# Odd layer: one store for several column blocks, a shorter boundary to the value projection, and an output projection that begins with the attention's half

## The chip, the cores and the metric

One core of one Trainium2 chip runs the whole program once per call. The metric is the device time in microseconds, from the first to the last instruction with what lies around them. Three runs of the kernel before gave a median of 3164.81 us, from 3162.14 to 3166.29.

## The reference, cut to what matters

Two layers of a decoder, for 2048 prompt positions and 8 sample tokens (2056 columns). The change lies in the second, the odd layer:

```python
proj = x @ w_in                      # 21 groups of 128 channels here, and a value projection of 1024
o_c  = stick_breaking(q_c, k_c, v_c) # attention, 512 channels; for the 8 samples over a paged cache
o_d  = gla_chunked(q_d, k_d, v_d, log_a)                      # gated recurrence, 512 channels
o_d  = o_d * rsqrt(mean(o_d * o_d) + eps) * gn_g              # per head of 128
out  = concat([o_c * silu(g_c), o_d * silu(g_d)]) @ w_out     # 1024 x 1024
x    = layer_norm(alpha * x + out)
```

The output projection sums over 1024 channels. The first 512 are the attention's and need nothing more when they are loaded; the last 512 need the norm of the recurrence and the gate.

## The kernel before, in words

The program is a chain of stages. Between two stages all engines meet: a stage ends when each engine has run its list of instructions, and then semaphores are cleared and the next stage begins. Buffers placed at fixed addresses, and some semaphores, outlive a stage, so that one stage can load or compute ahead for the next. Each engine's order is written out by hand.

A product in 32 bit is made of three TensorE passes over operands split into a high and a low part (`product`, lines 120 to 122: high by low, low by high, high by high). `high_part` is a copy (line 108), `low_part` a subtraction (line 113).

**Odd projection** (`project_odd`, tiles named po_). The weights of a group of 128 channels are multiplied with five blocks of columns (four of 412 and one of 408). There are 105 such slots, each of 24 matmuls, in the order of `ODD_GROUPS`; the first five share the loop over the contraction (`first`), and slots 5, 6 and 7 are all the last block, of three different groups. ScalarE evicts each slot's bank into one of four pieces of `po_o` (`evict`, line 1371) and issues its store (`store`, line 1310, 206 KB). Before it writes a piece it waits until the store of four slots ago has landed. Beside this runs the samples' attention. SP loads cache pages of keys for VectorE, and ScalarE loads pages of values for TensorE (line 2497, four pages of 256 KB, after the store of the same slot). For each sample the step goes: ScalarE's exponential at slot t, VectorE's clamp, ScalarE's logarithm at t+1 (line 2620), VectorE's maximum (line 2673), TensorE's triangle sum at t+2 (line 2559), VectorE's argument, ScalarE's exponential at t+3 (line 2625), TensorE's value sums from t+4 (line 2552). Here t is 22, 32, ... 92. The transposes that make the query rows (line 2577) come after slot 9 and need slot 7 evicted and VectorE's four memsets, which follow its split of weight group 4.

**Boundary to the value projection** (`project_values`, tiles pv_). When the last slot is done, SP issues `ValuesAhead.load`: tile 0 of x, four of eight slices of weights (`FRONT = 4`), tile 1 of x. Then it stores the samples' attention output into scratch `cat` (line 2534) and waits for it. The next stage begins with SP's other four weight slices, VectorE's split of tile 0 of x (`split_x`), then ScalarE's high parts and VectorE's low parts of the weights. TensorE starts when slice 0 is split. Tile 1 is split by VectorE after the last weight slice, and its low part is GpSimd's (line 113).

**Odd output projection** (`Tail`, tiles oo_). Block b of 256 columns holds `cat` with 8 slices: 0 to 3 the attention's, 4 to 7 the recurrence's. Weights are loaded and split, and block 0 is loaded, during the stage before (`gla_chunks`). In the stage itself TensorE first sums squares of the recurrence (`back(0)`, line 812), ScalarE makes the reciprocal root, VectorE scales (line 1120) and gates (line 1131) slices 4 to 7, and then `high(0)` and the low part split all 8 slices of tile 0. Only then `tile(0)` multiplies: 48 matmuls into two banks. `back(1)` and `tile(1)` follow. VectorE's order after that is: evict half of tile 0, scale block 1, evict the other half, split tile 2, normalise tile 0, evict tile 1, and so on.

Of the kernel before, what the change touches and what calls it, by code (L numbers as in the profile page):

```python
# [22 lines left out]
P = 128  # L23
D = 1024
KT = D // P
# [522 lines left out]
class Tail:  # L548
# [48 lines left out]
    def run(self):  # L597
        even = self.even
        with self.s as s:
# [19 lines left out]
            self.w_low = [s.sem("w_low_even"), s.sem("w_low_odd")]  # L619
            self.CST_B = 48 if even else 16  # L620
# [180 lines left out]
    def tensor(self, pe):  # L801
# [73 lines left out]
        def turned(t):  # L875
            if not self.even or t < 0:
                return
            h, n = t % 2, self.rows(t)
            pe.wait_ge(self.y_ok, t + 1)
            if t:  # L880
                pe.wait_ge(self.yT_ok, t)
            else:
                pe.wait_ge(self.lnc, 48)
            for k in range(KT):
                mm = pe.transpose(self.tr[:, k // 4, (k % 4) * P:(k % 4) * P + n], self.y[h][0:n, k * P:(k + 1) * P],
                                  self.idt[0:n, 0:n])
            mm.then_inc(self.tr_pe, 1)
        centre(0)
# [3 lines left out]
        if self.even:  # L892
            centre(1)
            glu(1, (0,))
        tile(0)
# [30 lines left out]

    def gpsimd(self, pool):
        def low(t):
            h, n = t % 2, self.rows(t)
            c = slice(h * P, h * P + n) if t < TT else slice(0, n)  # L930
            pool.wait_ge(self.c_high, t + 1)
            low_part(pool, self.cl[h][:, :, 0:n], self.cb[t // 2 % 2][:, :, c], self.ch[h][:, :, 0:n]).then_inc(self.c_low, 1)
        for t in range(1, TT + 1):
            low(t)
# [126 lines left out]
    def vector(self, dve):  # L1061
# [71 lines left out]
        def high(t):  # L1133
# [5 lines left out]
            high_part(dve, self.ch[h][:, :, 0:n], self.cb[t // 2 % 2][:, :, c]).then_inc(self.c_high, 1)  # L1139
# [48 lines left out]
        low_part(dve, self.cl[0][:, :, :], self.cb[0][:, :, 0:P], self.ch[0][:, :, :]).then_inc(self.c_low, 1)  # L1188
# [54 lines left out]
class Channels:  # L1243
# [7 lines left out]
    def __init__(self, s, xT, w, out, groups, banks, pinned=False):  # L1251
# [14 lines left out]
        self.kept = [s.sem(f"kept{n}") for n in range(self.PIECES)]  # L1266
# [3 lines left out]
        for t, (i, n, b) in enumerate(self.slot):  # L1270
            self.begin.setdefault(i, t)
        self.opens = {t: i for i, t in self.begin.items()}
        self.at = {(n, b): t for t, (i, n, b) in enumerate(self.slot)}

    def place(self, stage=None):
# [8 lines left out]
        self.ot = s.sb("o", [P, self.PIECES, BLK])  # L1284
        self.acc = [s.ps(f"acc{n}", [P, 512]) for n in range(self.banks)]

# [1161 lines left out]
def project_odd(nc, xT, w, z, cache_k, cache_v, table, bias, const, q_rows, cat, values_ahead):  # L2448
# [7 lines left out]
    with Stage(nc, "po") as s:  # L2456
# [16 lines left out]
         o_ev, o_pe, gate, out, stored) = (s.sem(n) for n in (  # L2473
             "cst", "tab", "q_tr", "q_ev", "q_st", "set", "prod", "k_used", "v_used", "biased", "exp", "cl", "ln",
             "sp", "tri_pe", "own", "arg", "att", "o_ev", "o_pe", "gate", "out", "stored"))
# [24 lines left out]
        def _(sp):  # L2500
# [33 lines left out]
            sp.dma_start(cat[0:4, :, SEQ:COLS].rearrange("n p c -> p n c"), oc[:, :, :]).then_inc(stored, 16)  # L2534
            sp.wait_ge(stored, 16)
# [51 lines left out]
        def _(act):  # L2587
# [8 lines left out]
            for t in range(TAIL):  # L2596
                if t < pj.slots:
# [6 lines left out]
                    pj.evict(act.copy, act, t, more)  # L2604
                    pj.store(act, t)
# [21 lines left out]
            for t in range(pj.slots - pj.PIECES, pj.slots):  # L2627
                pj.stored(act, t)

        @block.vector  # L2630
        def _(dve):
# [62 lines left out]
            for t in range(START, TAIL):  # L2694
# [10 lines left out]
                if t - PER - 3 in chain:  # L2705
# [4 lines left out]
                              gc[:, :, :].rearrange("p n b -> p (n b)"), ALU.mult).then_inc(out, 1)  # L2710

# [6 lines left out]
class ValuesAhead:  # L2718

    FRONT = 4  # L2720

    def __init__(self, nc, x, w):
# [9 lines left out]
        self.x_high, self.x_low = s.sem("x_high"), s.sem("x_low")  # L2732
# [8 lines left out]
    def load(self, sp):  # L2741
# [3 lines left out]
        self.tile(sp, 1)  # L2745
# [303 lines left out]
def project_values(nc, ahead, out, z, alpha_w, alpha_b, const, ops, wc, sample_vecs, scores):  # L3049
# [6 lines left out]
    with ahead.s as s:  # L3056
# [29 lines left out]
        def _(sp):  # L3086
# [43 lines left out]
            sp.wait_ge(late, 48)  # L3130
            for q in (0, 1):
# [104 lines left out]
        def _(dve):  # L3236
# [53 lines left out]
            ahead.split_x(dve)  # L3290
# [451 lines left out]
```

## Time and profile before

| | us |
|---|---|
| median of 3 runs | 3164.81 |
| the profiled execution's own time | 3165.45 |
| its span, first to last instruction | 3163.7 |
| TensorE matmul busy | 2913.2 (92%) |
| VectorE busy | 2101.6 (66%) |
| ScalarE busy | 1291.1 (41%) |
| mean granted TensorE clock | 0.969 |

The stages of the change lie at 1501 to 2137 us (odd projection), 2137 to 2348 (value projection) and 2936 to 3163 (odd output projection). Busy time is the union of an engine's instructions; an idle time in brackets stands before the instruction that ended it, with what released it.

### The profile page before, as it was taken

What the parts mean: (1) busy time and instruction counts of PE and PEld (TensorE: products, weight loads), DVE (VectorE), ACT (ScalarE), POOL (GpSimd) and SP (SyncE); (2) the same over time, 40 slices, a digit from 0 to 9 for tenths busy, and PEclk for the clock granted to TensorE, in tenths of its full rate; (3) what the DMA queues carried; (4) which work ended last, traced back from release to release, by engine and by line L of the source; (5) the groups of instructions that cost most, each with busy time, mean ns of one, the idle gap of its engine ahead of it and who ended that gap; (6) DMA issues with size and microseconds to landing.
All of it is one profiled execution on the core that took longest, in us unless ns stands there. A gap on an engine that the chain in (4) does not pass through costs nothing. (4 is left out here: it accounts for less than half of the span.)

```text
span 3163.7 us, 70060 instructions
## 1 busy us (share of the span) xinstructions
PE 2913.2 (92%) x27683; PEld 2367.9 (75%) x27683; DVE 2101.6 (66%) x3283; ACT 1291.1 (41%) x2293; POOL 724.9 (23%) x697
## 2 busy tenths in 40 slices
PE   8999999978898988998899999989989999998898
PEld 7899999967776766776887777877756666667676
DVE  9526666647666647885487677604639888887576
ACT  2225555434444435342310100012228888875332
POOL 5000000012232211110011111101227666664111
PEclk9999999989999989999999999999989999999999
DMA  6624545454443556552789999865450101008342
GB/s 214 204 95 151 154 151 153 140 162 117 105 116 87 130 150 195 158 174 84 260 253 342 319 330 322 294 192 170 149 193 6 68 14 55 15 20 257 124 158 77
DMA packets 470335, 502.83 MB, mean 159 GB/s; under 512 B 200065, under 2 KB 362866, under 8 KB 464986
## 3 DMA queue, kind: packets, MB, share of 16 engines
q1 hardware_dynamic: 373466, 339.83, 35.8%
q10 hardware_dynamic: 88032, 142.51, 13.0%
q0 software_dynamic: 8512, 16.02, 1.7%
q8 instruction: 221, 3.62, 0.5%
q14 instruction: 104, 0.85, 0.1%
HBM read 357.13 MB, written 141.31 MB: 158 GB/s over the span
## 5 line engine op out<-in xcount | busy, mean ns | idle before, releaser
L3029 POOL TENSOR_TENSOR sp_att<-sp_beta,sp_left 128x512 f32<-128x512 f32 (+3 forms) x320 | 302.3, 955 | 187.0 <-DVE sp_left L2990 172.6
L120 PE MATMUL po_acc<-po_x_high,po_w_low 128*128 128x412 f32 (+1 forms) x840 | 306.6, 365 | 15.1 <-DVE po_x_low L113 13.7
L120 PE MATMUL pe_acc<-pe_x_high,pe_w_low 128*128 128x412 f32 (+1 forms) x840 | 302.6, 360 | 5.4 <-PEq L86 5.4
L121 PE MATMUL po_acc<-po_x_low,po_w_high 128*128 128x412 f32 (+1 forms) x840 | 299.5, 357 | 0.0
L122 PE MATMUL po_acc<-po_x_high,po_w_high 128*128 128x412 f32 (+1 forms) x840 | 298.7, 356 | 0.0
L121 PE MATMUL pe_acc<-pe_x_low,pe_w_high 128*128 128x412 f32 (+1 forms) x840 | 293.7, 350 | 0.0
L122 PE MATMUL pe_acc<-pe_x_high,pe_w_high 128*128 128x412 f32 (+1 forms) x840 | 293.3, 349 | 0.0
L2990 DVE TENSOR_TENSOR_SCAN sp_left<-sp_z,sp_left,sp_zero 128x512 f32<-128x512 f32 x192 | 235.7, 1269 | 18.3 <-ACT sp_z L2951 14.0
L2654 DVE TENSOR_TENSOR po_work<-po_work,po_q 128x1024 f32<-128x1024 f32 x128 | 177.6, 1388 | 83.3 <-DMA po_work<-in_cache_k 74.4
L2943 ACT ACTIVATE sp_beta<-sp_z,sp_bias 128x512 f32<-128x512 f32 (+3 forms) x320 | 183.1, 628 | 94.1 <-PE sp_z L2881 47.7
L1371 ACT COPY po_o<-po_acc 128x412 f32<-128x412 f32 (+1 forms) x105 | 52.5, 500 | 392.2 <-PE po_acc L122 337.2
L120 PEld LDWEIGHTS po_acc<-po_x_high,po_w_low 128*128 128x128 f32 x840 | 162.4, 193 | 65.2 <-issue 33.1
L2430 POOL TENSOR_TENSOR rc_kt<-rc_kt,rc_mask 128x512 f32<-128x512 f32 x32 | 41.4, 1294 | 716.5 <-ACT rc_kt L2320 716.4
L2316 ACT COPY rc_lv<-rc_bk 128x1024 f32<-128x1024 f32 (+1 forms) x192 | 129.9, 693 | 181.1 <-DVE rc_f L2406 54.6
L2892 PEld LDWEIGHTS sp_t<-sp_id,sp_att 128*128 128x128 f32 x1088 | 117.4, 141 | 96.8 <-issue 89.8
L2951 ACT ACTIVATE sp_z<-sp_z,sp_bias_neg 128x512 f32<-128x512 f32 (+3 forms) x320 | 179.2, 610 | 0.0
L120 PEld LDWEIGHTS pe_acc<-pe_x_high,pe_w_low 128*128 128x128 f32 x840 | 158.4, 189 | 17.7 <-issue 16.5
L2878 PE MATMUL sp_z<-sp_k,sp_q 64*128 64x512 f32 (+3 forms) x640 | 164.0, 589 | 6.5 <-PEq L86 3.3
L2892 PE MATMUL sp_t<-sp_id,sp_att 128*128 128x128 f32 x1088 | 152.2, 279 | 17.5 <-ACT sp_aT L2957 16.6
L121 PEld LDWEIGHTS po_acc<-po_x_low,po_w_high 128*128 128x128 f32 x840 | 162.6, 194 | 0.9
L122 PEld LDWEIGHTS po_acc<-po_x_high,po_w_high 128*128 128x128 f32 x840 | 162.4, 193 | 0.7
L2909 PE MATMUL sp_ob<-sp_aT,sp_v 128*64 128x128 f32 x2176 | 154.7, 281 | 5.4 <-DVE sp_g L3004 5.4
(492 smaller groups left out, 6979.8 us busy)
## 6 DMA issues: line engine op xcount, KB each, us to landing
po_work<-in_cache_k SPq DMA_DIRECT2D x256, 256.0 KB, 4.8
po_work<-in_cache_v ACTq DMA_DIRECT2D x256, 256.0 KB, 4.6
scratch_ops<-pe_work SPq DMA_DIRECT2D x160, 128.0 KB, 2.0
out_z<-pe_o SPq DMA_DIRECT2D x84, 206.0 KB, 2.8
out_z<-po_o ACTq DMA_DIRECT2D x84, 206.0 KB, 4.2
pe_w<-in_w_e SPq DMA_DIRECT2D x21, 512.0 KB, 6.0
rc_opx<-scratch_ops SPq DMA_DIRECT2D x64, 160.0 KB, 3.7
po_w<-in_w_o ACTq DMA_DIRECT2D x20, 512.0 KB
```

Of the source, the lines that this page charges most:

```text
L120: pe.matmul(out, ll, rh, start=start, stop=False)
L121: pe.matmul(out, lh, rl, start=False, stop=False)
L122: return pe.matmul(out, lh, rh, start=False, stop=stop)
L2316: evict = lambda to, k, n: act.copy(lv[q][:, to:to + n].rearrange("p k x y c -> p x k (y c)"), b[:, :, 2 * k * CH:2 * (k + n) * CH].rearra ...
L2654: dve.tensor_tensor(kp[:, p % KR], kp[:, p % KR], qb[:, b % 2:b % 2 + 1, :].broadcast_to([P, 2, CW]), ALU.mult).then_inc(prod, 1)
L2878: mm[h] = pe.matmul(zb[h][b][:, 0:w], qt[q][r, cq], kt[q][r, ck], start=True, stop=not diagonal(n))
L2892: mm = pe.transpose(tb[h][:, b * P:(b + 1) * P], att[h][:, n % 3, b * P:(b + 1) * P], idt[:, :])
L2909: mm = pe.matmul(ob[tile(n) % 2][c, 0:P], vt[m % 2][:, 4 * g + b, c], aT[h][:, n % 2, b * P:(b + 1) * P], start=(diagonal(n) and b == 0), ...
L2943: act.activation(be[h][:, n % 4, 0:w], zb[h][n % 2][:, 0:w], ACT.Sigmoid, scale=DC ** -0.5, bias=bt[:, head:head + 1]).then_inc(sig[h], 1)
L2951: act.activation(zb[h][n % 2][:, 0:w], zb[h][n % 2][:, 0:w], ACT.Sigmoid, scale=-DC ** -0.5, bias=nbt[:, head:head + 1]).then_inc(kept[h], 1)
L2990: dve.tensor_tensor_scan(row[:, at:at + w][:, ::-1], zb[h][n % 2][:, 0:w][:, ::-1], zero.broadcast_to([P, w]), start, ALU.mult, ALU.add).t ...
L3029: pool.tensor_tensor(att[h][:, n % 3, 0:w], be[h][:, n % 4, 0:w], left[h][tile(n) % 2][:, at + 1:at + 1 + w], ALU.mult).then_inc(at_ok[h], 1)
```

## The change

1. Odd projection: `po_o` becomes one buffer of 2056 columns, with each block at its own columns. `runs` groups slots that follow each other in one weight group: blocks 0 and 1 make one store (412 KB), blocks 2 to 4 another (616 KB); a last block that stands alone is stored alone. `evict_run` waits for the latest store that covered this block.
2. Boundary: `FRONT` is 2, tile 1 of x is loaded in the next stage after the weights, the store of `cat` is waited for at the end of the next stage, and `split_x` is VectorE's last work in the odd projection.
3. Odd output projection: the attention's half of tile 0 (both halves of the output) and of tile 1 (the first) is split by VectorE before the norm, and multiplied by TensorE between `back(0)` and `tile(0)`. The later steps of these tiles take slices 4 to 7 only.

```diff
@@ Tail.tensor, tile(t)
-                if not self.even:
-                    pe.wait_ge(self.w_split, 2 * KT)
-                for k in range(KT):
+                for k in range(0 if self.even else 4, KT):
...
-                for k in range(KT):
+                for k in range(0 if self.even or u != 2 else 4, KT):
...
+        def attended():
+            pe.wait_ge(self.w_split, 2 * KT)
+            for t, halves in ((0, (0, 1)), (1, (0,))):
+                pe.wait_ge(self.a_low, t + 1)
+                for k in range(4):
+                    for q in halves:
+                        c = slice(q * 512, q * 512 + 512)
+                        product(pe, self.acc[2 * t + q][:, :], (self.ch[t][:, k, :], self.cl[t][:, k, :]),
+                                (self.wh[:, k, c], self.wl[:, k, c]), k == 0, False)
         centre(0)
         glu(0, (0,))
         back(0)
@@
+        else:
+            attended()
         tile(0)
@@ Tail: high and low parts of tiles 0 and 1 take these slices
+    def slices(self, t):
+        return slice(0, KT) if self.even or t > 1 else slice(4, KT)
@@ Tail.vector
+        def attended(t):
+            c, ks = slice(t * P, t * P + P), slice(0, 4)
+            if t == 0:
+                dve.wait_ge(self.b_in[0], self.loaded(0))
+            high_part(dve, self.ch[t][:, ks, :], self.cb[0][:, ks, c]).then_inc(self.a_high, 1)
+            dve.wait_ge(self.a_high, t + 1)
+            low_part(dve, self.cl[t][:, ks, :], self.cb[0][:, ks, c], self.ch[t][:, ks, :]).then_inc(self.a_low, 1)
@@
+        else:
+            attended(0)
+            attended(1)
         normed(0)
@@ Channels
+    def runs(self):
+        row, latest = [], {}
+        for t, (i, n, b) in enumerate(self.slot):
+            self.run_past[t] = latest.get(b)
+            row.append(b)
+            after = self.slot[t + 1] if t + 1 < self.slots else None
+            if after == (i, n, b + 1) and row != [0, 1]:
+                continue
...
+    def store_run(self, eng, t):
+        if t in self.run_end:
+            first, last = self.run_end[t]
+            lo, hi = first * BLK, min(COLS, (last + 1) * BLK)
+            eng.wait_ge(self.evicted, t + 1)
+            eng.dma_start(self.out[self.slot[t][1], :, lo:hi], self.ot[:, lo:hi]).then_inc(self.kept[first], 16)
+
+    def evict_run(self, copy, eng, t, more=()):
...
+        if self.run_past[t]:
+            first, count = self.run_past[t]
+            eng.wait_ge(self.kept[first], 16 * count)
+        eng.wait_ge(self.done, t + 1)
...
+        copy(self.ot[:, lo:hi], bank[:, 0:hi - lo]).then_inc(self.evicted, 1)
@@ project_odd, SP
-            sp.dma_start(cat[0:4, :, SEQ:COLS].rearrange("n p c -> p n c"), oc[:, :, :]).then_inc(stored, 16)
-            sp.wait_ge(stored, 16)
+            sp.dma_start(cat[0:4, :, SEQ:COLS].rearrange("n p c -> p n c"), oc[:, :, :]).then_inc(values_ahead.cat_put, 16)
@@ project_odd, ScalarE
-                    pj.evict(act.copy, act, t, more)
-                    pj.store(act, t)
+                    pj.evict_run(act.copy, act, t, more)
+                    pj.store_run(act, t)
@@ project_odd, VectorE, its last line
+            values_ahead.split_x(dve)
@@ ValuesAhead
-    FRONT = 4
+    FRONT = 2
@@ ValuesAhead.load
-        self.tile(sp, 1)
@@ project_values, SP
             for k in range(ahead.FRONT, KT):
                 ahead.weights(sp, k)
+            ahead.tile(sp, 1)
@@ its end
+            sp.wait_ge(ahead.cat_put, 16)
@@ project_values, VectorE
-            ahead.split_x(dve)
```

## Rows read from the trace of the kernel before

**Rows 1.** Windows of two stages: us, busy us of each engine (instructions), clock, DMA, GB/s.

```profile
1535.00:2125.00 590.00, 556.47 (x3017) 477.71 (x3015) 368.50 (x323) 61.37 (x137) 70.53 (x36) 0.97 0.86 288
2980.00:3163.00 183.00, 174.33 (x724) 131.04 (x724) 133.93 (x155) 58.14 (x84) 29.07 (x13) 0.98 0.37 122
```

**Rows 2.** Waits of PE, 1535 to 2125: engine, line, tile <- releaser: us, times, longest.

```profile
PE po_stat L2559 <- DVE po_softplus L2673: 15.5, 8, 6.5
PE po_sums L2552 <- ACT po_att L2625: 14.7, 7, 2.9
PE po_sums L2552 <- DMA po_work<-in_cache_v: 1.9, 2, 1.1
```

**Rows 3.** Timeline of ACT, one step of the odd projection: start us, duration, what [idle before].

```profile
1811.23 0.50 ACT L1371 COPY po_o<-po_acc 128x412 f32<-128x412 f32 x1
1811.76 0.36 ACTq L1310 DMA_DIRECT2D out_z<-po_o  x1
1812.83 3.78 ACTq L2497 DMA_DIRECT2D po_work<-in_cache_v  x4
1816.71 0.42 ACT L2620 ACTIVATE po_softplus<-po_e 128x256 f32<-128x256 f32 x1 [4.99 <-issue]
```

**Rows 4.** Timeline of PE at the two waits of the same sample.

```profile
1818.30 0.70 PE L2559 MATMUL po_stat<-po_softplus,po_tri 128*128 128x256 f32 x2 [1.51 <-DVE po_softplus L2673]
...
1831.61 1.06 PE L2552 MATMUL po_sums<-po_work,po_att 128*8 128x512 f32 x8 [2.04 <-ACT po_att L2625]
```

**Rows 5.** Windows after these two waits.

```profile
1818.00:1821.00 3.00, 2.71 (x15) 1.47 (x16) 3.00 (x2) 0.00 (x0) 2.41 (x1) 1.00 1.05 394
1833.00:1836.00 3.00, 3.00 (x14) 2.92 (x15) 2.13 (x2) 0.00 (x0) 0.00 (x0) 0.62 1.00 354
```

**Rows 6.** Timeline of PE near the stage's begin.

```profile
1561.56 0.60 PE L2577 MATMUL po_stat<-po_id,po_qc 128*8 128x128 f32 x4
```

**Rows 7.** Timeline of SP's queue at the boundary to the value projection.

```profile
2124.65 0.55 SPq L2736 DMA_DIRECT2D pv_x<-scratch_x1T  x1
...
2128.35 2.85 SPq L2534 DMA_DIRECT2D scratch_cat<-po_oc  x1
2137.85 1.76 SPq L2739 DMA_DIRECT2D pv_w<-in_w_v  x4
```

**Rows 8.** Windows at the same boundary.

```profile
2128.00:2132.00 4.00, 0.00 (x0) 0.00 (x0) 0.00 (x0) 0.00 (x0) 0.00 (x0) 0.84 1.06 412
2136.00:2138.00 2.00, 0.00 (x0) 0.00 (x0) 0.11 (x1) 0.14 (x1) 0.00 (x0) 0.50 0.00 0
```

**Rows 9.** Landings of the value projection's tiles of x, min/median/max.

```profile
DMA to landing us min/median/max: 4.2/4.8/8.7
```

**Rows 10.** Timeline of DVE and PE at the begin of the value projection.

```profile
2139.76 9.17 DVE L113 TENSOR_TENSOR pv_w_low<-pv_w,pv_w_high 128x1024 fp32r<-128x1024 f32 x8
...
2141.12 0.77 PE L120 MATMUL pv_acc<-pv_w_high,pv_x_low 128*128 128x512 f32 x1 [13.72 <-DVE pv_w_low L113]
```

**Rows 11.** Timeline of PE in the last stage.

```profile
2936.79 3.38 PE L812 MATMUL oo_part<-oo_rstd,oo_ones 128*128 128x512 f32 x4 [4.88 <-PEq L86]
2946.99 0.80 PE L120 MATMUL oo_acc<-oo_w_high,oo_cat_low 128*128 128x512 f32 x1 [6.82 <-DVE oo_cat_low L113]
...
2949.72 0.48 PE L120 MATMUL oo_acc<-oo_w_high,oo_cat_low 128*128 128x512 f32 x1
...
2959.36 1.88 PE L812 MATMUL oo_part<-oo_rstd,oo_ones 128*128 128x512 f32 x4
...
2980.06 3.26 PE L812 MATMUL oo_part<-oo_rstd,oo_ones 128*128 128x512 f32 x4 [2.19 <-ACT oo_rstd L957]
```

**Rows 12.** Timeline of DVE and POOL in the last stage.

```profile
2942.02 1.67 DVE L1120 SCALAR_TENSOR_TENSOR oo_cat<-oo_cat,oo_gn,oo_rstd 128x256 f32<-128x256 f32 x4 [5.29 <-ACT oo_rstd L987]
...
2945.71 1.23 DVE L113 TENSOR_TENSOR oo_cat_low<-oo_cat,oo_cat_high 128x1024 fp32r<-128x1024 f32 x1
...
2968.30 2.40 POOL L113 TENSOR_TENSOR oo_cat_low<-oo_cat,oo_cat_high 128x1024 fp32r<-128x1024 f32 x1 [18.19 <-DVE oo_cat_high L108]
```

More of the change, by code:

```diff
@@ L619, in run @@
             self.w_low = [s.sem("w_low_even"), s.sem("w_low_odd")]
+            self.a_high, self.a_low = s.sem("a_high"), s.sem("a_low")
             self.CST_B = 48 if even else 16
@@ L930, in low @@
             c = slice(h * P, h * P + n) if t < TT else slice(0, n)
+            ks = self.slices(t)
             pool.wait_ge(self.c_high, t + 1)
-            low_part(pool, self.cl[h][:, :, 0:n], self.cb[t // 2 % 2][:, :, c], self.ch[h][:, :, 0:n]).then_inc(self.c_low, 1)
+            low_part(pool, self.cl[h][:, ks, 0:n], self.cb[t // 2 % 2][:, ks, c], self.ch[h][:, ks, 0:n]
+                     ).then_inc(self.c_low, 1)
         for t in range(1, TT + 1):
@@ L1138, in high @@
                 dve.wait_ge(self.acc_pe, 2 * t - 2)
-            high_part(dve, self.ch[h][:, :, 0:n], self.cb[t // 2 % 2][:, :, c]).then_inc(self.c_high, 1)
+            ks = self.slices(t)
+            high_part(dve, self.ch[h][:, ks, 0:n], self.cb[t // 2 % 2][:, ks, c]).then_inc(self.c_high, 1)
+        def attended(t):
[5 more added lines that the diff above has]
+            low_part(dve, self.cl[t][:, ks, :], self.cb[0][:, ks, c], self.ch[t][:, ks, :]).then_inc(self.a_low, 1)
         def evict(t, q):
@@ L1187, in vector @@
         dve.wait_ge(self.c_high, 1)
-        low_part(dve, self.cl[0][:, :, :], self.cb[0][:, :, 0:P], self.ch[0][:, :, :]).then_inc(self.c_low, 1)
+        ks = self.slices(0)
+        low_part(dve, self.cl[0][:, ks, :], self.cb[0][:, ks, 0:P], self.ch[0][:, ks, :]).then_inc(self.c_low, 1)
         dve.wait_ge(self.c_low, 1)
@@ L1265, in __init__ @@
         self.done, self.evicted = s.sem("done"), s.sem("evicted")
-        self.kept = [s.sem(f"kept{n}") for n in range(self.PIECES)]
+        self.kept = [s.sem(f"kept{n}") for n in range(self.PIECES if pinned else NBLK)]
         self.slot = [(i, n, b) for i, (n, blocks) in enumerate(groups) for b in blocks]
@@ L1271, in __init__ @@
             self.begin.setdefault(i, t)
+        self.run_end, self.run_past, self.run_count = {}, {}, {}
+        if not pinned:
+            self.runs()
         self.opens = {t: i for i, t in self.begin.items()}
@@ L1283, in place, with runs_stored @@
             self.wh, self.wl = s.sb("w_high", [P, 2, KT * P]), s.sb("w_low", [P, 2, KT * P])
-        self.ot = s.sb("o", [P, self.PIECES, BLK])
+        self.ot = s.sb("o", [P, self.PIECES, BLK] if self.pinned else [P, COLS])
         self.acc = [s.ps(f"acc{n}", [P, 512]) for n in range(self.banks)]
+    def runs(self):
[6 more added lines that the diff above has]
+                continue
+            count = self.run_count[row[0]] = self.run_count.get(row[0], 0) + 1
+            for x in row:
+                latest[x] = row[0], count
+            self.run_end[t] = row[0], b
+            row = []
+    def store_run(self, eng, t):
[4 more added lines that the diff above has]
+            eng.dma_start(self.out[self.slot[t][1], :, lo:hi], self.ot[:, lo:hi]).then_inc(self.kept[first], 16)
+    def runs_stored(self, eng):
+        for first, count in self.run_count.items():
+            eng.wait_ge(self.kept[first], 16 * count)
+    def evict_run(self, copy, eng, t, more=()):
+        lo, hi = self.columns(t)
+        bank = self.acc[t % self.banks]
+        if self.run_past[t]:
+            first, count = self.run_past[t]
+            eng.wait_ge(self.kept[first], 16 * count)
+        eng.wait_ge(self.done, t + 1)
+        for dst in more:
+            copy(dst, bank[:, hi - lo - NS:hi - lo])
+        copy(self.ot[:, lo:hi], bank[:, 0:hi - lo]).then_inc(self.evicted, 1)
     def columns(self, t):
@@ L2472, in project_odd @@
         (cst, tab, q_tr, q_ev, q_st, set_, prod, k_used, v_used, biased, exp_, cl, ln, spl, tri_pe, own_, arg, att_ok,
-         o_ev, o_pe, gate, out, stored) = (s.sem(n) for n in (
+         o_ev, o_pe, gate, out) = (s.sem(n) for n in (
              "cst", "tab", "q_tr", "q_ev", "q_st", "set", "prod", "k_used", "v_used", "biased", "exp", "cl", "ln",
-             "sp", "tri_pe", "own", "arg", "att", "o_ev", "o_pe", "gate", "out", "stored"))
+             "sp", "tri_pe", "own", "arg", "att", "o_ev", "o_pe", "gate", "out"))
         k_in, v_in = [s.sem(f"k_in{n}") for n in range(KR)], [s.sem(f"v_in{n}") for n in range(VR)]
@@ L2626, in _ @@
             act.activation(gc[:, :, :], gc[:, :, :], ACT.Silu).then_inc(gate, 1)
-            for t in range(pj.slots - pj.PIECES, pj.slots):
-                pj.stored(act, t)
+            pj.runs_stored(act)
         @block.vector
@@ L2731, in __init__ @@
         self.w_low, self.x_in = [s.sem("w_low_even"), s.sem("w_low_odd")], [s.sem("x_in0"), s.sem("x_in1")]
-        self.x_high, self.x_low = s.sem("x_high"), s.sem("x_low")
+        self.x_high, self.x_low, self.cat_put = s.sem("x_high"), s.sem("x_low"), s.sem("cat_put")
     def tile(self, sp, t):
```

## The prediction

> **What bounds the kernel now.** I read the windows by stage first, then the waits of TensorE, and timelines only where these pointed. In both large stages of the change TensorE is nearly full: 556 of 590 us busy in the odd projection, 174 of 183 us in the later part of the odd output projection [rows 1]. So the change can win only what TensorE idles, and the clock that goes with it. There are three such places, and as they lie in different stages, with a meeting of all engines between them, their gains add.
>
> **Part 1, the odd projection.** The waits name who ends TensorE's idle time: eight waits for VectorE's softplus, 15.5 us, and seven for ScalarE's attention weights, 14.7 us [rows 2]. The timeline shows what these have in common. When a slot is done, ScalarE copies 0.50 us, issues the store for 0.36 us, begins its four page loads 1.60 us after the copy began, spends 3.78 us on them and only then computes its logarithm [rows 3]; TensorE, with 24 matmuls and a value sum to do meanwhile, comes 1.51 us too early. After the exponential three slots on it is 2.04 us [rows 4]. ScalarE's instructions at t, t+1 and t+3 fall on blocks 2, 3 and 0 of a group, and runs end at blocks 1 and 4. So each of these steps loses its store. What that is worth: at least the issue, 0.36 us with a gap of 0.03; at most also the copy's 0.50, if the registers for the page loads are read while the copy runs; 0.39 to 0.89. Nothing at all, if page loads and not the store hold the queue. I take 0.5, nearer to the issue, since the issue is certain to go. Of the softplus waits the first, 6.5 us, is VectorE's lateness and stays; seven remain, and 7 x 0.5 is 3.5 us. The attention waits give 7 x 0.5, again 3.5 us.
>
> The clock adds to this. After the wait of 2.04 us it was 0.62 of full speed, about its lower level, 1.2 GHz, for most of 3 us [rows 5]; after the wait of 1.51 us it was at full speed, 2.4 GHz [rows 5]. Where a wait falls from 2.0 to 1.5 us the loss may go. At 0.62 for 3 us, 1.1 us of full speed are lost; I put one loss at 0.5 to 1.5 us and count three of them gone at 1.0, which is 3 us, with none and six at 1.5 as ends. Part 1: 3.5 + 3.5 + 3 = 10 us; ends 0 and 21, of which 5.5 to 17 is what I believe.
>
> What it costs. Slots 5, 6 and 7 write the same columns, and each now waits for the store before it. The 616 KB store takes perhaps 6 us where 206 KB are in flight for 4 to 5, so ScalarE's load of weight group 4 comes some 4 us later, and with it VectorE's split and memsets. TensorE needs those at 1561.56 [rows 6]. By my count they are done within a microsecond of that. The banks don't bind: five of them give ScalarE four slots of slack. Cost 0.5, ends 0 and 3. The page loads of two slots out of five now stand behind a longer store on ScalarE's queue; TensorE waited for value pages only 1.9 us in the whole stage [rows 2], so there is slack, and I count 0 with 3 as an end. Net 9.5 us.
>
> The Trainium skill, Perfetto Trace Analysis, section DMA Optimizations, calls larger transfers the primary gain where a kernel is bound by DMA. The DMA engines are at 0.86 here [rows 1], but the waits put only 1.9 us on value pages, so by the rule the gain could be had from the pages, by the rows at most 1.9 us is there to gain. I follow the rows.
>
> **Part 2, the boundary.** The projection ends at 2124.65, when SP issues tile 0 of x, and the next stage's first load is at 2137.85 [rows 7]: 13.2 us. The samples' store, issued from 2128.35 to 2131.20, lies behind 3 MB of loads that run at 412 GB/s, and the traffic is over by 2136.00 [rows 8]; the stage then closes within 1.85 us. Afterwards 1.5 MB of loads are left in front (one tile, two slices), the last store grows from 204 to 616 KB, and the samples' store isn't waited for. The net 1.1 MB less are worth 2.7 us at 412 GB/s, the lower end. SP itself is through at about 2130.6 (its issue of 2.85 us, 0.6 us earlier), which with about 1 us for the meeting gives the upper end, 6.2 us. Between them stands VectorE: tile 0 lands 4.8 us after its issue, at worst 8.7 [rows 9], and its split is 0.69 and 1.23 us (the same shapes as in the last stage, [rows 12]). From 2124.65 + 6 + 2 + 1 the next stage begins at 2133.7. Gain 4.2 us; ends 1.5 and 6.2.
>
> Inside the value projection two things move. The split of x, 1.9 us, no longer stands ahead of the weights' low parts, which cost 9.17/8 = 1.15 us each [rows 10]; TensorE, which began 3.3 us after the stage, can begin after about 2.4, when ScalarE has cast slice 0 and VectorE has split it. That is 0.9 us. But tile 1 of x now lands behind six slices: 3.5 MB at 412 GB/s, about 11 us after the begin; VectorE is free at about 12.5, its cast and GpSimd's low part (2.40 us in the same shape, [rows 12]) make it ready at 15.9, and TensorE ends tile 0 at 15. So 0.9 is given back. Net 0, ends +1 and -2.
>
> **Part 3, the odd output projection.** TensorE sums squares from 2936.79 to 2940.17 and then idles 6.82 us, until the split of all eight slices; VectorE idles 5.29 us before it scales [rows 11, 12]. Added for VectorE: four instructions on 512 elements, two casts and two subtractions, at most 2 x (0.69 + 1.23) = 3.8 us by the full shape and about half of it, 2.1 us, by size: both fit in the 5.29, so they cost nothing. Without this cover they would delay the scaling by as much. Removed: half of the two splits after it, about 1 us.
>
> TensorE gets 36 matmuls at 2940.2. In the stage before the change the clock was low for six matmuls (2946.99 to 2949.72) and 42 more took 9.64 us, 0.23 each [rows 11]. After the sums at 2980.06, which began after a pause too, the clock rose about 4 us in. So from 2936.79 two of the 36 are slow at 0.43 and 34 take 7.8: the attention's half ends at 2948.9. The split of the other half is ready by 2946.1, so TensorE goes on: 24 matmuls, 5.5 us, and `back(1)` starts at 2954.4 instead of 2959.36. That is 5.0 us.
>
> Does the stage keep it? What comes late next is tile 2. VectorE works without a pause from the scaling of block 1 to the second eviction of tile 1, and that chain sets ScalarE's squares, which end the wait at 2980.06. It is started by `back(1)`, so it moves by 5.0. TensorE has 12 matmuls less, 2.8 us, in tile 1 and will wait for the split of tile 2 about 1.7 us, and again before the sums: time it has no use for. It arrives at the sums 5.0 us earlier, from where all is as before. The half of the first tile's work that lies beyond 5.0 is lost in those waits. Ends: 3, if the clock falls in them at a cost of 2 us, and 6.
>
> **Sum.** 9.5 + 4.2 + 0 + 5.0 = 18.7 us. From the profiled execution's 3165.45 (span 3163.7 and 1.75 around it) that gives 3146.8, and from the median, 0.64 lower, 3146.1. I say 3146.
>
> **Rivals.**
>
> A. The store isn't what ScalarE's steps wait for: the page loads' registers take as long either way. The 1.60 us from copy to first page load [rows 3] speak for it, as 0.71 of them lie after the store. Then part 1 gives 0 to 1, and the time is 3165 - 9 = 3156. Against: the queue runs in order and the 0.36 us are measured.
>
> B. The waits shrink further than I say, with the copy hidden and most of the clock's losses gone: 17 us from part 1, 3165 - 26 = 3139.
>
> C. The gain in the last stage is given back: TensorE's waits for tile 2 bring the low clock and VectorE, not TensorE, sets the pace after. Against: VectorE is 134 of 183 us busy there [rows 1]. Gain 1 instead of 5, 3150.
>
> D. Slower: the value pages behind the longer stores. In some 30 slots out of 72 with page loads, the store in front is 206 or 412 KB longer; at half of 412 GB/s, since keys load beside it, that is 1.0 or 2.0 us, together some 45 us if the pages had no slack. It decides from the point where pages land later than the two slots (11 us) between their load and their use. With half of it seen by TensorE: 3146 + 23 = 3169. The 1.9 us of waits [rows 2] speak against it.
>
> The Trainium skill, DMA: Bandwidth & Descriptors, section Queues, rings and completion order, says that a queue's descriptors are consumed in ring order and that an engine takes turns between queues packet by packet. By that the pages do wait for the store ahead of them, as D has it; no row shows the slack used up.
>
> **Chances.** My forecast, 3140 to 3152, 0.58; A 0.19; B 0.08; C 0.10; D 0.05. The range takes in A and nearly B: 3138 to 3158. A measurement can tell about 0.2%, 6.3 us, from no change: faster than that in my forecast, B, C and most of A, 0.93; within 0.04; slower 0.03.
>
> **What would show it.** Part 1: seven softplus waits of about 1.0 us instead of 1.5, attention waits of 1.5, fewer windows with a low clock; PE's idle time from 34 to about 27 us in that stage. Transposes of the query at 1562 or before. Part 2: the value projection's first load about 9 us after the last slot, its first matmul 2.4 us later, and TensorE waiting up to a microsecond at tile 1. Part 3: 36 matmuls from 3.4 us after the stage's first, no pause before tile 0, `back(1)` 17.6 us after the first instead of 22.6. I am wrong if the odd projection takes as long as before, if waits for in_cache_v grow to 10 us or more, or if the sums of block 2 come less than 4 us earlier in their stage.

## Result, and the profile after

The changed kernel took 3119.07 us (median of 4 runs, 3110.20 to 3123.61); the kernel before, run on the same chip, 3163.47 (3162.11 to 3166.29). The ratio is 0.9855, interval 0.9831 to 0.9879: 44 us less, where 18.7 were forecast. The time lies below the range. The profiled execution was the fastest of the four, 3110.20 us with a span of 3108.4, so a difference of two traces (55.3 us) is some 11 us more than one of the medians (44.4).

The starts of the named instructions cut both profiled spans into stretches (us).

| stretch | before | after | difference |
|---|---|---|---|
| up to the odd projection's first matmul | 1509.0 | 1505.0 | -4.0 |
| to the transposes of the query | 52.6 | 49.9 | -2.7 |
| to the first sum over softplus (sample 0) | 74.4 | 69.4 | -5.0 |
| to the projection's last matmul | 488.2 | 452.7 | -35.5 |
| to the value projection's first | 16.9 | 12.4 | -4.5 |
| to its last | 204.1 | 205.9 | +1.8 |
| to the odd output projection's first sum of squares | 591.6 | 592.1 | +0.5 |
| to the last output | 222.7 | 216.8 | -5.9 |

The first row is code that the change doesn't touch; it shows what two executions can differ by (over the traces of all kernels here it runs from 1502 to 1511 us). The fourth holds nearly all that the forecast lacks. What the third holds differs between executions of the same code, as is shown below. TensorE's waits and the stage's window, after, beside [rows 1, 2] (window: us, busy us of PE, PEld, DVE, ACT, POOL with instructions, clock, DMA share, GB/s):

```profile
PE po_sums L2618 <- ACT po_att L2691: 5.6, 7, 1.1
...
PE po_stat L2625 <- DVE po_softplus L2738: 1.5, 1, 1.5
```

```profile
1535.00:2080.00 545.00, 537.11 (x3000) 461.38 (x2998) 363.55 (x322) 61.38 (x133) 72.07 (x36) 1.00 0.89 309
```

Four things are to be seen. The seven later waits for softplus are gone; of sample 0's 6.5 us 1.5 are left. The attention's waits fell from 2.1 us each to 0.8. The granted clock is 1.00 over the window, where it was 0.97. Value pages aren't waited for at all (1.9 us before).

What ScalarE does in the same step as [rows 3], and three slots on:

```profile
1786.89 0.51 ACT L1352 COPY po_o<-po_acc 128x412 f32<-128x412 f32 x1 [0.68 <-PE po_acc L122]
1787.58 3.52 ACTq L2564 DMA_DIRECT2D po_work<-in_cache_v  x4
1791.20 0.42 ACT L2686 ACTIVATE po_softplus<-po_e 128x256 f32<-128x256 f32 x1 [3.81 <-issue]
...
1799.26 0.50 ACT L1352 COPY po_o<-po_acc 128x412 f32<-128x412 f32 x1 [6.15 <-PE po_acc L122]
1799.29 0.36 ACTq L1361 DMA_DIRECT2D po_w<-in_w_o  x1
1800.36 3.50 ACTq L2564 DMA_DIRECT2D po_work<-in_cache_v  x4
1803.96 0.42 ACT L2691 ACTIVATE po_att<-po_scores 128x256 f32<-128x256 f32 x1 [4.20 <-issue]
```

From the copy's begin to the first page load it is 0.69 us instead of 1.60. The last four lines show why: the weight load is issued 0.03 us after the copy began, while the copy runs. In the program a store of what the copy writes waits for the copy's semaphore, and everything behind the store on ScalarE's queue waits too.

The boundary, beside [rows 7, 10] (SP's queue, VectorE, TensorE):

```profile
2077.43 0.55 SPq L2802 DMA_DIRECT2D pv_x<-scratch_x1T  x1
2078.04 1.16 SPq L2805 DMA_DIRECT2D pv_w<-in_w_v  x2
2080.44 0.39 SPq L2601 DMA_DIRECT2D scratch_cat<-po_oc  x1
2086.97 2.83 SPq L2805 DMA_DIRECT2D pv_w<-in_w_v  x6
2089.85 0.53 SPq L2802 DMA_DIRECT2D pv_x<-scratch_x1T  x1
```

```profile
2083.90 0.69 DVE L108 CAST pv_x_high<-pv_x 128x1024 fp32r<-128x1024 f32 x1 [3.49 <-DMA pv_x<-scratch_x1T]
2084.63 1.23 DVE L113 TENSOR_TENSOR pv_x_low<-pv_x,pv_x_high 128x1024 fp32r<-128x1024 f32 x1
```

```profile
2089.43 0.77 PE L120 MATMUL pv_acc<-pv_w_high,pv_x_low 128*128 128x512 f32 x1 [9.25 <-DVE pv_w_low L113]
```

The next stage's first load is 9.5 us after the last slot (13.2 before) and its first matmul 2.5 us after that; VectorE's split of tile 0, which ends 1.1 us ahead of that load, is what came last, as forecast.

The last stage, beside [rows 11, 12]:

```profile
2887.42 3.41 PE L813 MATMUL oo_part<-oo_rstd,oo_ones 128*128 128x512 f32 x4 [4.88 <-PEq L86]
2890.18 0.88 PE L120 MATMUL oo_acc<-oo_w_high,oo_cat_low 128*128 128x512 f32 x1
```

```profile
2904.38 1.02 PE L813 MATMUL oo_part<-oo_rstd,oo_ones 128*128 128x512 f32 x2
```

```profile
2892.68 1.67 DVE L1135 SCALAR_TENSOR_TENSOR oo_cat<-oo_cat,oo_gn,oo_rstd 128x256 f32<-128x256 f32 x4 [3.17 <-ACT oo_rstd L1002]
```

TensorE goes on without a pause, `back(1)` comes 16.96 us after the first sum instead of 22.57, and VectorE's scaling isn't later (5.26 us after the first sum, 5.23 before).

### The profile page after: what moved, and what is told of

It is laid out like the page before. It is cut to its first block and busy times, and to the rows that moved or that the text cites. A ratio compares the mean times of both kernels' runs of the same rounds, so it can differ in the third digit from the quotient of the medians.

```text
span 3108.4 us, 70002 instructions
## 1 busy us (share of the span) xinstructions
PE 2894.9 (93%) x27683; PEld 2354.0 (76%) x27683; DVE 2100.7 (68%) x3287; ACT 1292.6 (42%) x2293; POOL 724.8 (23%) x697
## 5 line engine op out<-in xcount | busy, mean ns | idle before, releaser
L1352 ACT COPY po_o<-po_acc 128x412 f32<-128x412 f32 (+1 forms) x105 | 52.5, 502 | 374.7 <-PE po_acc L122 329.2
L121 PEld LDWEIGHTS pe_acc<-pe_x_low,pe_w_high 128*128 128x128 f32 x840 | 158.6, 189 | 1.4
L2722 DVE TENSOR_REDUCE po_scores<-po_work 128x16 f32<-128x1024 f32 x128 | 156.4, 1222 | 4.4
## 6 DMA issues: line engine op xcount, KB each, us to landing
out_z<-pe_o SPq DMA_DIRECT2D x84, 206.0 KB, 2.8
```

The costliest lines, as they stand in the source:

```text
L121: pe.matmul(out, lh, rl, start=False, stop=False)
L2722: dve.tensor_reduce(zs[b % 2][:, :, r:r + 2].rearrange("p h r -> p r h"), kp[:, p % KR].rearrange("p j (h c) -> p j h c", c=DC), AX.X, ALU ...
```

## Experiments

All ratios are against the kernel before on the same chip: 3166.34 us for the first four, 3165.65 for the next four, 3163.66 for the last three. The first three do one part of the change alone.

**1. The stores alone.** The kernel before with part 1.

> Part 1 alone (merged stores), parts 2 and 3 as before. In the traces the odd projection's slots took 43 us less than before. Theory Q (the 206 KB store behind the eviction's copy held ScalarE's queue) and theory D (larger stores cost the DMA engines less) both put nearly all of it here: about 3127 us, PE's waits in the odd projection 34 us before, 8 here, granted clock 1.00 there. The prediction's size of part 1, 9.5 us, gives 3154. A theory that the gain came from a lucky run of the profile gives 3150 or more.

3133.33 us (3131.27 to 3137.95), ratio 0.9898, 0.9872 to 0.9924: 33.0 us less, more than part 1's upper end of 21. TensorE's waits for the attention were 5.4 us, nearly as in the whole change (5.6). The time lies 6 us above what theories Q and D gave and 21 below what the prediction's size gave; this run can't tell Q from D. One cost of part 1 shows at the stage's end: with the last store grown to 616 KB and the boundary as it was, the value projection's first matmul came 19.1 us after the last one of the projection, where it was 16.9.

**2. The boundary alone.** The kernel before with part 2.

> Part 2 alone (two weight slices ahead, tile 1 later, the store of cat waited for a stage later, x split before the boundary). By the trace of after: last slot to the value projection's first load 13.2 us before, 9.5 us here with the 616 KB last store; here that store is 204 KB, so x lands at 5 to 6.5 us and the boundary is 8 to 9.5 us. First tile 1 us longer. Sum: 3160 to 3162, gain 1.5 to 3.5. The prediction's 4.2 gives 3159.5.

3160.39 us, ratio 0.9984, 0.9970 to 0.9999: 6.0 less. From the last matmul of the projection to the first of the value projection it was 10.9 us, where it was 16.9. The interval is 0.3 to 9.5 us, so the time alone hardly tells the gain from nothing; the trace's 6.0 us speak for it.

**3. The attended half alone.** The kernel before with part 3.

> Part 3 alone (the attention's half ahead of the norm). The last stage keeps 5.6 us (trace of after), the prediction said 5.0: 3158. If the last stage's gain in the trace of after depended on the other parts: 3163.

3157.75 us, ratio 0.9968, 0.9954 to 0.9982: 8.6 less (5.7 to 14.6 by the interval), where the trace's last stage shows 4.3 (218.4 us instead of 222.7). The parts sum to 47.6 and the whole gave 44.4: within the intervals they add. The forecast is short by part 1.

**4. Small stores, issued late.** The kernel before with its 105 stores of 204 to 206 KB, but each at the head of the next slot, ahead of its eviction (shown against the changed kernel; parts 2 and 3 are left out).

```diff
-                    pj.evict_run(act.copy, act, t, more)
-                    pj.store_run(act, t)
+                    if t:
+                        pj.store(act, t - 1)
+                    pj.evict(act.copy, act, t, more)
```

> The stores stay as before, 105 of 204 to 206 KB, but each is issued ahead of the next slot's eviction instead of behind its own copy, so that it goes out while ScalarE waits for TensorE. Parts 2 and 3 as before. Theory Q: page loads begin 0.7 us after the copy began instead of 1.6, waits fall as with merged stores, 3125 to 3132. Theory D (size of the transfers): no change, 3160 to 3165. If both: between.

3135.81 us (3128.46 to 3149.82), ratio 0.9903, 0.9877 to 0.9928: 30.5 less, which can't be told from the 33.0 of the joined stores. ScalarE's step, to be read beside [rows 3]:

```profile
1798.13 0.50 ACT L1435 COPY po_o<-po_acc 128x412 f32<-128x412 f32 x1 [0.96 <-PE po_acc L122]
1799.38 3.78 ACTq L2561 DMA_DIRECT2D po_work<-in_cache_v  x4
1803.26 0.42 ACT L2687 ACTIVATE po_softplus<-po_e 128x256 f32<-128x256 f32 x1 [4.62 <-issue]
1803.28 0.36 ACTq L1374 DMA_DIRECT2D out_z<-po_o  x1
```

The store is now behind the logarithm. From the copy to the page loads it is 1.25 us in these rows, not the 0.7 that were expected, and the time is 4 us above theory Q's range. What counts is when the logarithm begins: counted from its slot's last matmul, in the mean of samples 1 to 7, that was 5.6 us before, 4.8 here and 4.5 in the changed kernel; for the attention's exponential it was 6.1, 4.8 and 4.8. So theory D's "no change" is out: neither the number nor the size of the transfers has to change for the gain. That no store stands between a chain step's copy and its page loads brings it.

**5. Joined stores, on the chain's slots again.** The changed kernel with stores of block 0, blocks 1 and 2 joined, block 3 and block 4 (84 stores instead of 63).

```diff
-            if after == (i, n, b + 1) and row != [0, 1]:
+            if after == (i, n, b + 1) and b == 1:
```

> The changed kernel with the stores' blocks joined otherwise: block 0, blocks 1 and 2, block 3 and block 4 (84 stores instead of 63), each still right behind its own copy. So stores stand again in the slots in which ScalarE does the recurrence's and the attention's chain. Theory Q (a store right behind its own copy holds ScalarE's queue, in the chain's slots, for the copy and for what follows): TensorE's waits for softplus and attention come back, some 30 us in the projection, and with them the lower clock: about 3145 to 3155. Theory S (fewer and larger transfers bring the gain): 84 stores are nearer to 63 than to 105, half or more of the gain of 33 us stays: 3119 to 3135.

3160.92 us (3149.87 to 3166.72), ratio 0.9983, 0.9969 to 0.9996. Parts 2 and 3 are still in, and alone they gave 6.0 and 8.6 us; the gain of part 1 is gone. The time is longer than either theory gave, 6 us above the upper end of Q and 26 above that of S. TensorE's waits and a step of ScalarE:

```profile
PE po_stat L2625 <- DVE po_softplus L2738: 19.7, 8, 8.9
...
PE po_sums L2618 <- ACT po_att L2691: 13.4, 7, 2.2
```

```profile
1809.65 0.48 ACT L1352 COPY po_o<-po_acc 128x412 f32<-128x412 f32 x1
1810.16 0.35 ACTq L1337 DMA_DIRECT2D out_z<-po_o  x1
1811.24 3.50 ACTq L2564 DMA_DIRECT2D po_work<-in_cache_v  x4
```

Both waits are about those of the kernel before (15.5 and 14.7 us; 8.9 of the 19.7 are sample 0's), and the 1.59 us from copy to page loads are its 1.60. Theory S falls. The place of the store is the cause, shown in both directions by experiments 4 and 5.

**6 and 7. The attention's exponential made late.** The changed kernel with three, and with six, exponentials of 64 columns ahead of it, each waiting for the one before.

```diff
+                    for _ in range(3):
+                        act.activation(idle[:, :], flat(zs[b % 2])[:, 0:64], ACT.Exp).then_inc(idled, 1)
+                        idles[0] += 1
+                        act.wait_ge(idled, idles[0])
                     act.activation(flat(att), flat(zs[b % 2]), ACT.Exp).then_inc(att_ok, 1)
```

> The changed kernel (3119.1 us) with three exponentials of 64 columns, each waiting for the one before, put on ScalarE ahead of the attention's exponential of each of the eight samples; their results are used by nobody. Estimated 0.25 to 0.35 us each with its wait, so TensorE's wait at each attention grows by about 0.9 us, from 0.4-1.1 to 1.3-2.0 us. Theory W (waits cost their length and nothing more): 8 x 0.9 = 7 us, so about 3126, granted clock in the odd projection stays 1.00. Theory C (each such wait of about 2 us is followed by a stretch at the lower clock, as in the kernel before, where 15.5 us of the odd projection went that way): 7 us of waits and up to 8 x 2 = 16 us of clock, so 3130 to 3142, granted clock of the chain's stretch 0.97 to 0.99.

> The same with six exponentials in each sample, some 1.8 us, so that TensorE's wait at the attention becomes 2.2 to 2.9 us, as long as or longer than in the kernel before (2.04 to 2.1). Theory W: 8 x 1.8 = 14 us over the changed kernel, about 3133, granted clock 1.00. Theory C: 14 us of waits and about 2 us of lower clock behind each, 16 us: about 3149, granted clock of the chain's stretch about 0.97 as in the kernel before.

Three: 3132.44 us (3128.21 to 3138.38), ratio 0.9893, 0.9873 to 0.9913. Six: 3151.68 us (3146.67 to 3156.35), ratio 0.9949, 0.9931 to 0.9966. By the ratios that is 12 and 30 us over the changed kernel, where the waits themselves grew by 5.8 and 11.8 us. With six, both the time and the trace say theory C. With three, the intervals (some 10 us either way on the difference) don't exclude theory W by themselves; the trace does, with 10.9 us lost to the clock where the changed kernel lost none. The waits with six, and two stretches of 12 us behind such a wait (us, busy us of PE, clock, DMA share, GB/s):

```profile
PE po_sums L2619 <- ACT po_att L2696: 17.4, 7, 2.8
```

```profile
1704.93:1716.93 12.00, 12.00 (x72) 1.00 0.90 291
1947.31:1959.31 12.00, 12.00 (x49) 0.61 0.83 266
```

In both TensorE is busy all the time; in the second it starts 49 matmuls instead of 72, and loses 12 x 0.39 = 4.7 us. Wait by wait for samples 1 to 7, with the mean clock of the 4 us from 1 us after the released matmul began:

| kernel | attention waits in order, us | clock behind each |
|---|---|---|
| before | 2.60, 1.82, 2.04, 2.02, 2.91, 2.02, 1.28 | 0.53, 0.65, 0.64, 0.63, 0.64, 0.50, 1.00 |
| three | 1.63, 1.64, 1.66, 1.95, 1.65, 1.63, 1.25 | 1.00, 1.00, 1.00, 0.50, 0.57, 0.66, 1.00 |
| six | 2.49, 2.51, 2.50, 2.52, 2.78, 2.51, 2.11 | 1.00, 0.60, 0.50, 0.50, 0.50, 0.52, 0.50 |

In these three kernels the clock went to its lower level after 13 of 14 waits of 1.8 us and more. The traces of all kernels here hold more such waits of TensorE between the transposes and the projection's last matmul, and some went the other way: after waits of 1.8 to 2.9 us the lower level followed in 27 of 32, after all nine longer ones, after 1.6 to 1.8 us in 3 of 9, and after the 90 of at most 1.54 us never. The changed kernel has none above 1.5.

**8. The pauses filled.** The kernel before, with 10 matmuls of 412 columns ahead of the wait for the attention and 6 ahead of that for softplus; nobody uses what they give.

```diff
                 if first:
-                    pe.wait_ge(att_ok, b + 1)
                     pe.wait_ge(o_ev, b)
+                    fill(sums, 10)
+                    pe.wait_ge(att_ok, b + 1)
@@ later(b)
-                pe.wait_ge(spl, b + 1)
+                pe.wait_ge(q_ev, 1)
                 pe.wait_ge(arg, b)
+                fill(stat, 6)
+                pe.wait_ge(spl, b + 1)
```

> The kernel before, its stores and all else unchanged, with matmuls of 412 columns that nobody uses put on TensorE right ahead of its two waits in each of the eight samples: 10 ahead of the wait for the attention, 6 ahead of the wait for softplus. At a pitch of 0.17 us they fill 1.7 and 1.0 us of waits that took 2.1 and about 1.2 us, so TensorE arrives later but is released at the same instants. Theory C (15 us of the odd projection's time in the kernel before are the lower clock that follows the pauses, and not the pauses themselves): the pauses go from the list of waits though the chain is no earlier, the granted clock of the chain's stretch rises from 0.97 to 1.00, and the time falls by 8 to 15 us, to 3150 to 3157. Theory W (the clock is low there for another reason, or follows the chain): 0.97 stays, and the time is that of the kernel before or up to 5 us more: 3165 to 3170.

3155.13 us (3150.04 to 3165.42), ratio 0.9969, 0.9953 to 0.9986: 8.5 less (4.4 to 14.9), in spite of 128 matmuls more. Its waits, and two windows of the stage (columns as above):

```profile
PE po_stat L2567 <- DVE po_softplus L2681: 10.7, 7, 8.4
...
PE po_sums L2558 <- ACT po_att L2633: 2.0, 4, 0.8
```

```profile
1875.00:1925.00 50.00, 50.00 (x281) 1.00 0.95 337
1925.00:1975.00 50.00, 48.85 (x275) 1.00 0.97 329
```

The chain is no earlier, since the stores still stand in it; only the clock is back (3.5 us are lost to it, against 15.3 before, by the table below). The time that TensorE stood still is now filled and not won. That separates the two halves of the gain.

**9 to 11. Toward a faster one.** The changed kernel again; it with the attention's exponential ahead of its slot's page loads; and that with the value projection's tile 1 of x issued after four of the six weight slices.

```diff
+                if t - 3 in chain:
+                    b = chain[t - 3]
+                    ...
+                    act.activation(flat(att), flat(zs[b % 2]), ACT.Exp).then_inc(att_ok, 1)
                 for g in at(groups, t - 1):
@@ project_values, SP
                 ahead.weights(sp, k)
-            ahead.tile(sp, 1)
+                if k == 5:
+                    ahead.tile(sp, 1)
```

> The changed kernel itself, on the same chip as the next one: 3119 expected (3110 to 3124 seen). A repeat for comparison; the two theories say the same.

> The changed kernel with ScalarE's exponential of the attention moved ahead of the page loads that its slot issues (3.5 us of ScalarE's queue every slot). Theory Q': ScalarE's queue sets the remaining waits of TensorE for the attention (7 of them, 5.6 us): they go, and the gain is 5 us, about 3114. Rival V: what ends last there is VectorE's and GpSimd's scores ahead of the exponential, ScalarE just waits for them with the page loads behind it: the waits stay, the page loads come later, and the time is 3119 or up to 10 us more where value pages are then waited for.

> The changed kernel with ScalarE's attention exponential ahead of the page loads of its slot, and SyncE's load of the value projection's second tile of x issued after four of the six remaining weight slices instead of after all six. Theory R (TensorE's remaining waits of 0.8 us for the attention are ScalarE's page loads, and the value projection's first tile loses 1 us to the late second tile of x): 5.6 and up to 1 us less than the changed kernel on the same chip, 3112 to 3114. Rival: other work of the same length takes their place (the attention's wait was 0.8 us of which the next slot's work hides none, but the weight slices come 1 us later): no difference from the changed kernel beyond 2 us.

3119.57 us (3109.57 to 3121.27), ratio 0.9858, 0.9834 to 0.9883; 3115.48 (3115.20 to 3123.24), 0.9849, 0.9828 to 0.9870; 3119.29 (3108.87 to 3127.88), 0.9861, 0.9834 to 0.9887. With the exponential first, TensorE waits no longer for the attention, and ScalarE waits for VectorE's scores instead:

```profile
ACT po_att L2678 <- DVE po_scores L2746: 6.7, 7, 2.0
```

That took the attention's 5.6 us away, but two waits for softplus, 3.2 us together, came in their place, and the stretch from the first softplus sum to the projection's last matmul fell by only 2.5 us, 452.7 to 450.2. The time lies 1.5 us above theory Q' and 3.5 below rival V; the intervals are wider than the 5 us between them, so it decides nothing. With tile 1 earlier the value projection took 207.1 us instead of 205.9, and TensorE waited 1.7 us for that tile, where it didn't wait before: nothing gained. The time of 3119.29 is what R's rival gave, but that execution also had a sample 0 wait of 4.9 us and lost 3.1 us to the clock. The three can't be told apart, so Q' and R are not shown and not refuted.

## Why the prediction was wrong

The step that failed is the size of part 1: 3.5 + 3.5 us for the waits that part 1 shortens and 3 us for the clock. Alone it gave 33.0 us where 9.5 net were forecast; by its trace 18.7 us are waits and 13.7 are clock. The mechanism behind both terms, a store that holds ScalarE's queue and a clock that falls after waits of about 2 us, was the right one.

The account of the odd projection closes within 3 us for every kernel. From the trace: the stretch from sample 0's softplus sum to the last matmul, TensorE's waits in it, and the time lost to the clock, which is the sum of (1 - clock) x length over windows of 4 us. Sample 0's wait lies ahead of the stretch and has the last column.

| kernel | stretch | waits | clock | rest | sample 0's wait |
|---|---|---|---|---|---|
| before | 488.2 | 25.6 | 15.3 | 447.3 | 6.5 |
| changed | 452.7 | 5.6 | 0.0 | 447.1 | 1.5 |
| changed, again | 452.8 | 5.8 | 0.0 | 447.0 | 1.5 |
| stores alone | 455.8 | 6.9 | 1.6 | 447.3 | 5.0 |
| boundary alone | 485.8 | 23.5 | 15.4 | 447.0 | 1.5 |
| attended half alone | 485.5 | 23.6 | 14.6 | 447.3 | 7.5 |
| small stores, late | 458.2 | 8.1 | 1.7 | 448.4 | 9.8 |
| stores on the chain's slots | 487.3 | 25.1 | 15.1 | 447.1 | 8.9 |
| three exponentials | 467.9 | 11.4 | 10.9 | 445.6 | 4.7 |
| six | 484.1 | 17.4 | 22.2 | 444.5 | 4.1 |
| pauses filled | 480.6 | 6.5 | 3.5 | 470.6, of it 122 x 0.19 = 23 added | 8.4 |
| exponential first | 450.2 | 3.2 | 0.0 | 447.0 | 0 |
| exponential first, tile 1 earlier | 450.4 | 0.7 | 3.1 | 446.7 | 4.9 |

In this stretch the change gained 20.0 us of waits and 15.3 of clock.

- **The store's place was the right step, its size was wrong.** I bounded what a chain step gains by 0.39 to 0.89 us and took 0.5, "nearer to the issue". The traces show 0.91 (1.60 to 0.69 from copy to page loads). The copy is hidden, as the upper bound had it: page loads' preparation goes on while the copy runs, and only a store of the copied data stops it. The rows of before left both ends open; the bound's upper end, 0.89, was the right one. In the slot of the attention a weight load stands there too, and the stretch fell from 2.35 to 1.10, by 1.25 us; the attention's waits fell by 9.1 / 7 = 1.30. The row of the same slot before, beside the lines of after above:

```profile
1825.19 0.50 ACT L1371 COPY po_o<-po_acc 128x412 f32<-128x412 f32 x1 [7.60 <-PE po_acc L122]
1825.72 0.36 ACTq L1310 DMA_DIRECT2D out_z<-po_o  x1
1826.12 0.44 ACTq L1294 DMA_DIRECT2D po_w<-in_w_o  x1
1827.54 3.50 ACTq L2497 DMA_DIRECT2D po_work<-in_cache_v  x4
```

  The seven softplus waits went whole. They were 9.0 us together, 1.3 each; the forecast took them for 1.5 each, from one row [rows 4]. The logarithm began 1.1 us earlier after its slot's last matmul (4.5 for 5.6): 0.9 is the stretch from copy to page loads, and the rest is the copy itself, which began 0.34 us after that matmul in the kernel before and 0.09 us in the changed one. ScalarE had come late out of the slot in front, which held a store too.
- **The clock's term was wrong by a factor of five.** I counted three losses of 1.0 us. Before, six attention waits out of seven and sample 0's wait were followed by the lower level, and the mean clock of the 12 us behind them was 0.72 to 0.87: 1.6 to 3.4 us each, 15.3 in all. The prediction's window of 3 us [rows 5] shows 1.1 us lost, where the 12 us behind the same wait, at 0.86, show 1.7, and [rows 1] held the answer unused: 0.97 over 590 us is 17 us. All of it went, with waits of 0.4 to 1.1 us left. Experiments 6 and 7 bring it back with nothing but a late exponential, and experiment 8 takes 12 of the 15.3 us away while the chain stays late. Rival B was the nearest and still short, 17 us where part 1 measured 33.
- **"Of the softplus waits the first is VectorE's lateness and stays": not decided.** It was 6.5 us before and 1.5 in both runs of the changed kernel, but that isn't the stores' doing as far as the runs show. With the boundary alone, where the odd projection's stores are the old ones, it was 1.5 too. Six traces (changed, changed again, both with late exponentials and both with the exponential first) have the same program up to this wait, and in them it was 1.5, 1.5, 4.7, 4.1, 0 and 4.9. So it differs by up to 5 us between executions, and the 5.0 us of the third row of the first table can't be put down to part 1. What sets it was not tried and stays open.
- **The costs of part 1 inside the stage were not seen.** The transposes come 49.9 us into the stage, not later than before (52.6; the kernels with joined stores have 49.9 to 52.5, the others 52.1 to 53.6), and value pages, rival D's case, are waited for 0 us. The Trainium skill, DMA: Bandwidth & Descriptors, section Queues, rings and completion order, says that a DMA engine consumes a queue's descriptors in ring order. No run here shows the order of descriptors. The order of the issues is seen in the rows, and what it cost was the wait for the copy, not the bytes in front of the pages. The Trainium skill, Perfetto Trace Analysis, section DMA Optimizations, calls batching small transfers into larger ones the primary optimization for a kernel that is DMA-bound. This stage waits for pages 1.9 us in all, and size isn't what gained: 105 small transfers in the right place gave 30.5 us, 84 partly larger ones in the wrong place took part 1's gain away.
- **Part 2 held.** 4.5 us against 4.2 forecast, 9.5 us from the last slot to the next load against 9, first matmul 2.5 us later against 2.4. The samples' store took 0.39 us to issue instead of 2.85. Inside the value projection 0 was forecast; 205.9 us stands against 204.1 before, but the stores alone, where this stage is the old one, also took 206.0, so nothing is shown to have changed there. The wait of up to a microsecond at tile 1 didn't come in the changed kernel; with part 2 alone it was 0.9 us. Part 2 alone gave 6.0 us, 0.3 to 9.5 by its interval. The working calls 2.7 us the lower end and goes on with 1.5; nothing hangs on it.
- **Part 3 held.** 5.9 us in the trace, 4.3 when alone, against 5.0. The first of the 36 matmuls began 2.8 us after the stage's first, not 3.4; `back(1)` came after 17.0 us, not 17.6.
- **The rivals and the range.** A (the store isn't what holds) is refuted by experiments 4 and 5, C (the last stage gives its gain back) by that stage's trace. The range is said to take in B nearly; with B at 3139 and the lower end at 3138 it takes it in whole, and the measured time lies below both.

## What to carry to other kernels

On an engine that both computes and issues DMAs, look for a DMA that needs the result just computed: it holds back everything queued behind it until that instruction is done, here 0.9 us for a copy of 0.5 and an issue of 0.36. Moving it behind the next urgent step gave the time back, for stores of 206 KB as for larger ones. Before pricing short waits of TensorE, multiply the stage's length by what its mean clock lacks: that is the most that the clock can give back. In this stage nearly all of it belonged to recurring waits of about 2 us and went with them. Where a wait couldn't be shortened, matmuls that nobody uses, put ahead of it, kept the clock up, and here they paid for themselves (8.5 us).

## What the runs showed of the hardware

- ScalarE issued a DMA that doesn't depend on its running copy 0.03 us after that copy began (the weight load at 1799.29). One that does waited for the copy and added 0.9 us to what is behind it (1.60 us against 0.69 from copy to page loads).
- A pause of TensorE of 1.8 to 2.9 us in the odd projection was followed in 27 of 32 cases by a stretch at the lower clock, which cost 1.7 to 4.7 us of the 12 us behind the pause. None of the 90 pauses of at most 1.54 us was. What tells the five exceptions apart is open. The fall can come late: behind the pause that ended at 1893.15 in the kernel before, the clock was full for 2 us more.
- The issue of the same store of the samples' columns took SyncE 2.85 us before and 0.39 in the changed kernel, with 1.5 MB less ahead of it. The other kernels divide the same way: 2.9 to 5.0 us with the old boundary, 0.39 with the new one.
